# A chunked recurrence scan: four-quadrant matmuls for z, values and the solved product, a key exchange by ScalarE, and two turns moved ahead of z

## The reference, cut to what matters

```python
def wkv_scan(s0, r, decay, k, v, kk, b, reverse, emit):
    def step(s, inp):
        r_t, w_t, k_t, v_t, kk_t, b_t = inp
        sa = jnp.einsum('bhij,bhj->bhi', s, kk_t)
        s = s * w_t[:, :, None, :] - sa[..., None] * b_t[:, :, None, :] + v_t[..., None] * k_t[:, :, None, :]
        y = jnp.einsum('bhij,bhj->bhi', s, r_t) if emit else None
        return s, y
    s_final, ys = lax.scan(step, s0, xs, reverse=reverse)
```

## Time and profile before

| | us |
|---|---|
| runs of the kernel | 3148.9, 3151.34, 3152.78 (median 3151.34) |
| the profiled execution, its own time | 3147.49 |
| its span | 3145.5 |
| mean granted TensorE clock of the span | 0.948 |

### The profile page before, as it was taken

How to read it: one execution, slowest core, us unless ns; L and a number is a source line. 1 busy time by engine, 2 the same in 40 slices (tenths; PEclk the granted TensorE clock), 3 DMA queues, 4 the chain that set the end, 5 groups by cost and what they waited for, 6 DMA issues and landing times. The chain is left out here.

```text
span 3145.5 us, 53318 instructions
## 1 busy us (share of the span) xinstructions
PE 2830.0 (90%) x22982; PEld 2186.0 (69%) x22982; DVE 1532.7 (49%) x2519; ACT 1067.0 (34%) x1932; POOL 132.7 (4%) x122
## 2 busy tenths in 40 slices
PE   6799888999979998879999988898887988899997
PEld 2488765777768886358887876566566766788876
DVE  6623247344546666674554243554535436445422
ACT  6411267332224443213222232554224132422222
POOL 0000000000013452000000000000000000000000
PEclk9899999999989999989999989999888999999999
DMA  9411200134100002202332323212111122233321
GB/s 317 131 54 54 51 2 1 54 113 141 44 1 4 4 4 79 78 24 76 100 95 90 94 61 124 82 53 75 48 60 38 48 89 66 67 88 94 99 85 64
DMA packets 221643, 224.37 MB, mean 71 GB/s; under 512 B 27360, under 2 KB 192736, under 8 KB 221345
## 3 DMA queue, kind: packets, MB, share of 16 engines
q1 hardware_dynamic: 221106, 219.78, 23.1%
q10 hardware_dynamic: 304, 1.18, 0.1%
HBM read 207.61 MB, written 12.80 MB: 70 GB/s over the span
## 5 line engine op out<-in xcount | busy, mean ns | idle before, releaser
L212 DVE TENSOR_TENSOR second_w_low<-second_w_raw,second_w_high 128x1024 fp32r<-128x1024 f32 (+1 forms) x236 | 282.2, 1198 | 488.3 <-ACT second_w_high L208 487.6
L208 ACT CAST second_w_high<-second_w_raw 128x1024 fp32r<-128x1024 f32 (+1 forms) x236 | 241.5, 1025 | 684.1 <-PE ffn_in_acc L233 246.7
L231 PE MATMUL ffn_in_acc<-ffn_h_high,second_w_high 128*128 128x512 f32 x704 | 279.6, 397 | 5.2 <-DVE ffn_h_low L670 4.6
L232 PE MATMUL ffn_in_acc<-ffn_h_low,second_w_high 128*128 128x512 f32 x704 | 277.2, 394 | 0.0
L233 PE MATMUL ffn_in_acc<-ffn_h_high,second_w_low 128*128 128x512 f32 x704 | 277.0, 394 | 0.0
L212 DVE TENSOR_TENSOR first_w_low<-first_w_raw,first_w_high 128x1024 fp32r<-128x1024 f32 x91 | 110.4, 1220 | 240.1 <-ACT first_w_high L208 240.0
L231 PEld LDWEIGHTS ffn_in_acc<-ffn_h_high,second_w_high 128*128 128x128 f32 x704 | 133.2, 189 | 37.0 <-issue 7.4
L231 PE MATMUL attn_in_acc<-attn_h_high,first_w_high 128*128 128x256 f32 (+1 forms) x416 | 143.9, 346 | 15.4 <-DVE attn_h_low L406 15.4
L208 ACT CAST first_w_high<-first_w_raw 128x1024 fp32r<-128x1024 f32 x91 | 94.4, 1045 | 186.2 <-PE attn_in_acc L233 80.5
L232 PEld LDWEIGHTS ffn_in_acc<-ffn_h_low,second_w_high 128*128 128x128 f32 x704 | 133.3, 189 | 29.5 <-issue 0.7
L233 PEld LDWEIGHTS ffn_in_acc<-ffn_h_high,second_w_low 128*128 128x128 f32 x704 | 133.2, 189 | 29.5
(11 more groups left out here) (828 smaller groups left out, 6308.3 us busy)
## 6 DMA issues: line engine op xcount, KB each, us to landing
second_w_raw<-in_ffn_w_gate SPq DMA_DIRECT2D x44, 512.0 KB, 3.8
second_w_raw<-in_ffn_w_up SPq DMA_DIRECT2D x44, 512.0 KB, 3.8
second_w_raw<-in_ffn_w_down SPq DMA_DIRECT2D x40, 512.0 KB, 3.5
first_w_raw<-in_rec_w_in SPq DMA_DIRECT2D x33, 512.0 KB, 4.1
second_w_raw<-in_w_in SPq DMA_DIRECT2D x24, 512.0 KB, 3.9
second_w_raw<-in_w_branch_gate SPq DMA_DIRECT2D x24, 512.0 KB, 4.1
first_w_raw<-in_attn_w_in SPq DMA_DIRECT2D x22, 512.0 KB, 3.9
first_w_raw<-in_attn_ada_w SPq DMA_DIRECT2D x12, 512.0 KB, 7.6
```

The lines of the kernel that those rows point to most:

```text
L208: act.copy(self.view(self.high[b % self.splits], b), self.view(self.raw[self.ring[b]], b)).then_inc(self.high_done, 1)
L212: dve.tensor_tensor(self.view(self.low[b % self.splits], b), self.view(self.raw[self.ring[b]], b), self.view(self.high[b % self.splits], b ...
L231: pe.matmul(out, sh, mh, start=(first and j == 0), stop=False)
L232: pe.matmul(out, sh, ml, start=False, stop=False)
```

## The change

1. z, the values and the solved product use all four quadrants instead of two. For `h = 1`, z now comes out in the partitions of the other chunk, so do the values, and so the solved product reads both crossed and writes its result uncrossed, where it lay before.
2. The values go to columns 256 to 511 of both banks of `late`, beside z, instead of bank 1 of `sa_ps`. Therefore `value` now waits for ScalarE's copy of z.
3. The way (turned keys times z) needs, for `h = 1`, the keys in the partitions of z. ScalarE's copy of the turned keys, one copy of 128 by 512, becomes three: 128 by 256 for `h = 0`, and two of 64 by 256 for `h = 1` that exchange the upper and the lower half of the partitions.
4. `turn0` and `turn1` move on TensorE from behind z to ahead of z and of its waits. ScalarE's order stays: z, then turn0, turn1, turn2.

```diff
-RWKV_PE = Marks("four", "step4", "eight", "step8", "step16", "ux", "mh", "wx", "gram_k", "z", "turn0", "turn1", "turn2",
+RWKV_PE = Marks("four", "step4", "eight", "step8", "step16", "ux", "mh", "wx", "gram_k", "turn0", "turn1", "z", "turn2",
                 "value", "solved", "way")
@@ halved(n)
-                pe.wait_ge(act_done, RWKV_ACT(n, "wx0"))
-                pe.wait_ge(dve_done, RWKV_DVE(n, "wx1"))
-                tiles(late, 0, wx[:, 1], wx[:, 0], 0, 0).then_inc(pe_done, 1)
                 if n and outs(n - 1):
                     pe.wait_ge(out_act, outs(n - 1))
                 turn(n, 0, bank(out_ps, 0))
                 turn(n, 2, bank(out_ps, 1))
+                pe.wait_ge(act_done, RWKV_ACT(n, "wx0"))
+                pe.wait_ge(dve_done, RWKV_DVE(n, "wx1"))
+                tiles(late, 0, wx[:, 1], wx[:, 0], 0, 1).then_inc(pe_done, 1)
                 turn(n, 3, bank(sa_ps, 0))
@@ value(n)
                 pe.wait_ge(dve_done, RWKV_DVE(n, "gram_k1"))
+                pe.wait_ge(act_done, RWKV_ACT(n, "z"))
...
-                            r, to = rows(k), (4 * h + i) * CH
-                            ins = pe.matmul(sa_ps[r, BANK + to:BANK + to + CH], gk[dr][r, h, i, 0, :], vt[r, tile, at:at + CH],
+                            r, to = rows(k), h * BANK + 256 + i * CH
+                            ins = pe.matmul(late[rows(k ^ h), to:to + CH], gk[dr][r, h, i, 0, :], vt[r, tile, at:at + CH],
@@ solved(n)
-                tiles(late, 0, z, av, 0, 0).then_inc(pe_done, 1)
+                tiles(late, 0, z, av, 1, 0).then_inc(pe_done, 1)
...
-                            ins = pe.matmul(sa_ps[rows(h), at:at + CH], tok[dr][rows(k), 0, i, rows(h)], z[rows(k), h, i, :],
+                            r = rows(k ^ h)
+                            ins = pe.matmul(sa_ps[rows(h), at:at + CH], tok[dr][r, 0, i, rows(h)], z[r, h, i, :],
@@ scalar queue
-                act.copy(wide(tok[dr][:, 0]), bank(out_ps, 0)).then_inc(act_done, 1)
+                heads, turned = (a.rearrange("p i (h t) -> p h i t", h=2) for a in (
+                    tok[dr][:, 0], bank(out_ps, 0).rearrange("p (i t) -> p i t", t=P)))
+                act.copy(heads[:, 0], turned[:, 0])
+                act.copy(heads[rows(0), 1], turned[rows(1), 1])
+                act.copy(heads[rows(1), 1], turned[rows(0), 1]).then_inc(act_done, 1)
...
-                act.copy(all_of(av), bank(sa_ps, 1)).then_inc(act_done, 1)
+                act.copy(by_bank(av), both(late, 256)).then_inc(act_done, 1)
```

## The result

The changed kernel takes 3160.72 us (median of 20 runs), the kernel before 3147.55 us (20 runs on the same chip): a ratio of 1.0037, 95% interval 1.0029 to 1.0046. It is 0.37% slower, some 12 us, where 8 us of gain was forecast. The profiled execution took 3153.51 us, with a span of 3151.6 us where the earlier trace rows has 3145.5.

A forecast was written before the change was run, and what follows sets the result against it. TensorE's tail was taken to bound each recurrence group, VectorE 0.50 us behind. Gains 5 x 0.69 + 5 x 0.77 + 0.89 + 0.7 = 8.9 us, less 0.9 allowance, gave 3151.3 - 8.0 = 3143.3 us; range 3140.5 to 3148.5.

The forecast's parts named there:

- the overlap at the end of a group: TensorE's tail sets a group's end, VectorE's chain only 0.50 us behind; faster products gain 0.69 to 0.89 us a group.
- The copies' price: ScalarE's three copies of the turned keys: 0.26 us each, 0.78 in all, 0.29 more than the single copy.
- Rival B: ScalarE's queue holds the grams, through 0.38 us copies or slower mode switches: 4.9 us gained, 3146.4 us; chance 0.20.
- the prediction's own sign of being wrong: Grams waiting for ScalarE beyond 2.3 us, a new same-size VectorE wait, or more than one clock fall, 940 to 1225 us.
- Solved: Solved product over four quadrants: first matmul to ScalarE's copy 0.69 + 0.04 us instead of 1.35, 0.62 less.
- Turns ahead of z: turn0 and turn1 on TensorE before z fill 0.6 us of waiting and push z back 0.4 us.
- z's quadrants: z over four quadrants takes 0.69 us in place of 1.15; with the moved turns it ends only 0.06 us earlier.
- The switch of tiling mode: Two more TensorE tiling switches a group, 0.15 to 0.20 us per switch, already counted in the sum.
- The last group: Group without following grams: value's copy starts 0.23 us earlier, solved to way's copy about 1.2 instead of 1.69; 0.7 us gained.
- rival C: Shorter TensorE bursts make the clock fall, about 1.3 us each; 3157 if every group; chance 0.09 few, 0.04 nearly every group.
- Rival D: Four quadrants don't speed z and solved, while copies add 0.29 us: 2.4 us slower, 3153.7 us; chance 0.05.

The follow-up runs named there:

- the first shift: Changed kernel with 64 already satisfied waits (32 more TensorE instructions in the trace) ahead of group 0, so block boundaries fall elsewhere: ratio 1.0030.
- the thinned pair: Changed kernel and kernel before, each computing the in-chunk part of the output for one pair of four: ratios 1.0026 and 0.9994 to the kernel before.

## Why the prediction was wrong

Mean times over the groups 0 to 10, in us, each from the first start of one burst or instruction to the first start of the next; before is the mean of two profiles, the changed kernel that of four, "clean" its median over the groups of its first profile, with the square's last step taken as in the kernel before:

| step | before | forecast | changed, clean | changed, mean |
|---|---|---|---|---|
| gram_k to z | 1.57 | 1.94 | 2.01 | 2.09 |
| z to its copy | 1.21 | 0.73 | 0.76 | 0.77 |
| z's copy to the grams | 2.22 | 2.01 to 2.09 | 2.37 | 2.37 |
| grams to solved | 1.70 | 1.70 | 1.65 | 1.67 |
| solved to its copy | 1.35 | 0.73 | 0.92 | 1.17 |
| copy to square | 0.64 | 0.64 | 0.64 | 0.83 |
| square to VectorE's additions | 1.29 | 0.73 to 0.9 | 1.23 | 1.56 |
| sum | 9.98 | | 9.58 | 10.46 |
| additions to the next gram_k | 14.61 | 14.6 | | 14.92 |

**The step that failed** is the overlap at the end of a group: that because "TensorE runs from z at 1070.03 without a real pause" in group 5, a faster product ends earlier, the whole tail moves up, and after it "the next group has the same order and lengths". The reading of group 5 is right. What failed is carrying it to faster products with a term of nothing for the supply of instructions. I took the pace of a single burst, 0.015 us a matmul, and carried it over products that follow one another. It holds within a burst, but a block of 256 instructions could not be had more often than every 3.3 to 3.5 us, and at four-quadrant pace it is used up in less (0.69 us for 64 instructions, at most 2.8 for a block). The signs were in the trace of before: some 10 us of idle weight loading put down to `issue`, nearly all of it outside the tail that the prediction reads, and the queue of instructions with 67 packets. Neither stands in the prediction. Clean groups of the changed kernel gain 0.30 us (9.88, the median of before, to 9.58), 3.3 us in 11. The stalls then add 0.88 us a group between gram_k and VectorE where before had 0.10: 8.6 us. That last is a difference of means, and part of it is clock, below. The second count of the stalls agrees: 0.85 us before and 8.5 changed in this part of the groups, 7.6 more.

**The copies' price** was mis-sized: forecast 0.26 us each from a 128x256 copy of another stage, measured 0.38. The grams thus start 0.15 us later after z's copy instead of up to 0.2 earlier; with z's start that makes 0.32 us a group, 3.5 us. Rival B had this mechanism and 0.38 with it, and the prediction's own sign of being wrong, grams beyond 2.3 us, came true; but its sum, 3146.4, fails for the same reason as mine. The run with one copy says that the three cost more in the whole than this 3.5 us, some 9. By the 186 ns + 0.833 ns an element and 93 ns of overlap of the Trainium skill ("ScalarE: Activation LUTs", section "What ACT_TABLE_LOAD costs") an estimate for 256 elements back to back is 306 ns; here the three took 0.38 us, and no overlap shows. The measurement decides.

**Solved** gains 0.43 us, not 0.62, in a clean group. The first of its matmuls still starts among the grams' last (the lines at 1083.15 to 1083.35 above, with gram matmuls of line 2534 between them), so the burst doesn't begin at its full pace.

**Turns ahead of z** came out: 2.01 against 1.94 us from gram_k to z. z's quadrants: 0.76 against 0.73. The switch of tiling mode, from the start of turn1's last transpose (1078.15) to z at 1078.36, took 0.21 us where the sum had 0.20.

**The last group** gains 0.38 us from z's copy to the way's (4.88 to 4.50), forecast 0.7.

**The clock**, rival C, played a small part. Between the two z's the kernel before shows one stretch of 3.4 us at the 1.2 GHz level in one profile and none in the other, the changed kernel two stretches in two profiles and one in two. By the prediction's 1.3 us for one, that is some 1.3 us of the loss. The one of the first profile of the changed kernel, as a window of 1 us (the granted clock stands before the last two columns):

```profile
1203.00:1204.00 1.00, 1.00 (x48) 1.00 (x44) 0.00 (x0) 0.97 (x4) 0.98 (x1) 0.50 0.00 0
```

Rival D is out: z and the values take 0.69 us, and solved 0.85 in most groups where before it had 1.31.

**The account**: 3.3 us won in the clean groups, 8.6 lost on the way to VectorE's additions, 3.4 (11 x 0.31) between them and the next gram_k: 8.7 us slower by the profiles, against 12 [9, 15] by the timed runs; the rest lies within what profiles of one kernel differ by (the window differed by 4.6 us between the two of before).

What is shown: 128 further instructions a group in the pause cost 26 us and as much engine time in 32 instructions 4, so the supply is a limit of this kernel; 128 fewer, with slower products, give back what the change lost; one copy in place of three gives back some 9 of the 12 us; the loss stays wherever the blocks begin. What is argued only: that the loss of the change is mainly supply. For it stand the second count of the stalls, 7.6 us more on the way to the additions and 2.9 of the 3.4 us behind them; against it stand the run with one copy, the first shift and the thinned pair, all of which the supply theory forecast otherwise. What stays open: how the 12 us divide between the supply and the copies, and why 96 fewer instructions in the output part gave 3 us and not 5 to 10.

## What to carry to other kernels

Before making bursts of small matmuls faster, count the instructions: look at the queue of instructions in the DMA view and at idle time put down to `issue` inside a burst. Where those show, a faster pace can turn into waits, fewer and wider instructions may be worth more, and a pause filled with small products is not free. Take the price of a copy from a row with the same neighbours, not only the same size.

## What the runs showed of the hardware

- TensorE's instructions arrive in packets of 16 KB, one for every 253 to 258 matmuls and weight loads, on a queue of their own, never less than 3.2 us apart in any of the profiles, and mostly over 3.3.
- TensorE goes on from a stall some 2.5 us after the start of a packet: 340 of 356 irregular idle stretches end 2.15 to 2.95 us after one. Of the 356, 269 end 0.95 to 1.55 us before the next.
- An fp32 matmul of 64x64x64 counts four instructions (two matmuls, two weight loads), so 64 of these products are one block.
- Three copies of 256 elements from PSUM by ScalarE follow each other at 0.38 us, on 128 and on 64 partitions alike, while copies of 512 elements of 0.59 us follow at 0.48.
